# A two-layer decoder trunk in fp32 from split operands: six orders changed, and the first up-projection step's weights made ready early

## The reference, cut to what matters

```
for l in range(2):                                   # x: 1024 prompt rows and 8 x 8 sample rows, D = 1024
    h = x @ w_in[l]                                  # 1792 columns: z_u, z_v, q, k, v
    A = gelu(z_u) * (W_spatial . LN(gelu(z_v)) + b)  # gMLP in chunks of 128 positions
    B = sliding-window attention(rotary(q), rotary(k), v, sinks)   # samples against a cache of 128
    x = LN(alpha * x + concat(A, B) @ w_out[l])
    up = x @ w_up[l]                                 # 2 x 2816 columns, then causal conv of width 3
    x = LN(alpha * x + (gelu(conv(g)) * conv(u)) @ w_down[l])
```

## Time and profile before

| | us |
|---|---|
| median of 3 runs | 2398.47 (2396.57 to 2401.55) |
| the profiled execution | 2398.07 |
| its span in the trace | 2396.3 |
| PE busy | 2244.6 (94%) |
| DVE busy | 1655.8 (69%) |
| ACT busy | 980.8 (41%) |
| POOL busy | 782.8 (33%) |

### The profile page before, as it was taken

How to read it: one execution, slowest core, us unless ns; L and a number is a source line. 1 busy time by engine, 2 the same in 40 slices (tenths; PEclk the granted TensorE clock), 3 DMA queues, 4 the chain that set the end, 5 groups by cost and what they waited for, 6 DMA issues and landing times.

```text
span 2396.3 us, 35859 instructions
## 1 busy us (share of the span) xinstructions
PE 2244.6 (94%) x14276; PEld 2025.5 (85%) x14276; DVE 1655.8 (69%) x2014; ACT 980.8 (41%) x1773; POOL 782.8 (33%) x444
## 2 busy tenths in 40 slices
PE   7999899799999999999999998987999999999996
PEld 7997677699999998887799876767999999987875
DVE  1558747777777776777636586486777777767777
ACT  2227634543443444333412375454344344443332
POOL 1115234434434440220311342344443444402202
PEclk9999989899999999999999999998999999999999
DMA  5412145122222224755551213541222222255762
GB/s 149 99 29 64 57 152 164 45 83 66 73 83 71 68 83 151 276 201 183 188 132 45 56 38 102 144 152 45 65 74 83 69 70 83 83 222 197 249 213 95
DMA packets 207974, 269.50 MB, mean 112 GB/s; under 512 B 31952, under 2 KB 166584, under 8 KB 207736
## 3 DMA queue, kind: packets, MB, share of 16 engines
q1 hardware_dynamic: 207808, 267.21, 36.5%
HBM read 217.39 MB, written 46.13 MB: 110 GB/s over the span
## 4 chain that ended last, share of the span: by engine, by line
PE 56%; DVE 20%; ACT 7%; issue 5%; DMA 4%; POOL 4%; SPq 2%; DVEq 0%; ACTq 0%; POOLq 0%
PE ps L2056 23%; PE ps L1770 13%; PE ps L1735 9%; PE ps L1995 3%; DMA wblk<-in_w_up 3%; DVE rl L1424 2%; POOL bl L733 2%; SPq L528 2%; DVE bnst L1252 1%; DMA wrow<-in_w_down 1%; POOL wblk L741 1%; PE ps L1795 1%; ACT bh L938 1%; PE ps L1874 1%; DVE bl L1356 1%
## 5 line engine op out<-in xcount | busy, mean ns | idle before, releaser
L2056 PE MATMUL ps<-bt,bh 128*128 128x272 f32 x3520 | 598.2, 292 | 29.9 <-issue 19.7
L2056 PEld LDWEIGHTS ps<-bt,bh 128*128 128x128 f32 x3520 | 503.5, 191 | 37.3 <-issue 25.9
L938 ACT ACTIVATE bh<-wblk 128x512 fp32r<-128x512 f32 x308 | 183.6, 624 | 542.8 <-POOL wblk L745 237.5
L2056 PE MATMUL ps<-bt,bl 128*128 128x272 f32 x1760 | 367.3, 290 | 0.0
L1356 DVE TENSOR_TENSOR bl<-wblk,bh 128x512 fp32r<-128x512 f32 x210 | 165.2, 803 | 182.2 <-ACT bh L938 182.2
L2056 PEld LDWEIGHTS ps<-bt,bl 128*128 128x128 f32 x1760 | 278.7, 191 | 0.0
L733 POOL TENSOR_TENSOR bl<-wblk,bh 128x512 fp32r<-128x512 f32 x98 | 163.3, 1669 | 310.8 <-ACT bh L938 310.8
L1770 PE MATMUL ps<-rh,ah 128*128 128x512 f32 x792 | 246.3, 392 | 14.7 <-DVE rzd L1238 6.5
L2056 PE MATMUL ps<-ba,bh 128*128 128x272 f32 x1408 | 238.4, 292 | 9.0 <-POOL bl L733 4.1
L1770 PE MATMUL ps<-rl,ah 128*128 128x512 f32 x792 | 244.1, 389 | 0.0
L1424 DVE TENSOR_TENSOR rl<-wrow,rh 128x1024 fp32r<-128x1024 f32 x132 | 191.6, 1452 | 51.0 <-ACT rh L994 51.0
(11 more groups left out here) (223 smaller groups left out, 4081.4 us busy)
## 6 DMA issues: line engine op xcount, KB each, us to landing
wrow<-in_w_down SPq DMA_DIRECT2D x132, 512.0 KB, 4.7
wblk<-in_w_up SPq DMA_DIRECT2D x88, 512.0 KB, 5.2
a_scr<-hg SPq DMA_DIRECT2D x44, 552.0 KB, 3.4
araw<-a_scr SPq DMA_DIRECT2D x88, 192.0 KB, 4.5
wrow<-in_w_out SPq DMA_DIRECT2D x48, 256.0 KB, 5.5
wrow<-in_w_out SPq DMA_DIRECT2D x24, 512.0 KB, 4.0
wraw<-in_w_in SPq DMA_DIRECT2D x10, 1024.0 KB, 6.0
z_scr<-rzc SPq DMA_DIRECT2D x16, 512.0 KB, 3.7
```

What stands on the lines that cost most here:

```text
L938: act.activation(bh[b][:], block_of(f, b), ACT.Copy).then_inc(S["u_hi"], 1)
L2056: e = nc.tensor.matmul(out[:, n, :], lhs, rhs[:, HW_ // 2 * n:HW_ // 2 * n + HW_ // 2], start=(k == 0 and m == 0), stop=(k == HK - 1 and m ...
```

## The change

Seven things are edited. They change no arithmetic.

1. Samples: the second transposes, the keys and the scores come one block later on PE, the transposes of the probabilities and the values after the first and the second tile of the tail of group 0; ACT's exponentials move from kk = 5 to kk = 6.
2. Norm turns: PE's `turn_z` in groups 1 and 2 comes after kk = 1, 3, 5 instead of 0, 2, 4, and what ACT does with it also one kk later. The product nmr is written as a tensor_scalar.
3. The operands of group 2 on DVE: the next tile's `turned` stands ahead of a tile's `operand_lo`.
4. Keys: the three operations of `keys` stand at gMLP blocks 4, 5 and 6, not all at 5.
5. gMLP: PE does chunk (3, 2) and chunk (4, 0) ahead of block 0's transposes, so each block has the two chunks that follow; the last has one.
6. Residuals: in the down-projection the join of a group's third tile stands ahead of `act_lo` and `down_lo`.
7. Step 0's weights: SP loads them at c = 21 of the output projection into a part of `btf` that tiles 6 and 7 use later. ACT copies B_11 and B_12 at kk = 4 and 5 of group 2; POOL subtracts them after row blocks 20 and 21 and makes two of the four sums after block 22, ahead of block 23. DVE's sums for tiles 6 and 7 wait until those weights are used.

```diff
@@ -369,7 +369,23 @@
+            if f == 0 and b in (B_11, B_12, B_22):
+                return quarter(which, k0)
             return wblk[s0 + which][:, k0:k0 + HK, :]
+
+        def quarter(which, k0):
+
+            return btf[:, 32 - 8 * which + k0:36 - 8 * which + k0, first_cols(NB - 1)]
+
+        def split_of(f, b):
+
+            if f:
+                return bh[b], bl[b]
+            if b < B_S2:
+                r, cols = 32 - 8 * b, first_cols(NB - 2)
+                return bt[:, r:r + HK, cols], bt[:, r + HK:r + 8, cols]
+            i = {B_S2: 0, B_S1: 1, B_S3: 2, B_22: 3, B_S4: 6}[b]
+            return bh[i], bl[i]
...
                 if f == 0:
-                    sp.wait_ge(S["w_lo"], l * WIO + INT + OUTU - 2)
+                    sp.wait_ge(S["c_done"], l * NTOK + 6)
...
-                        elif c < OUTU + 2:
-                            up_cols(l, c - OUTU)
+                        elif c == OUTU:
+                            up_cols(l, 1)
+                        if c == OUTU - 3:
+                            up_cols(l, 0)
...
+            def sum_first(l, b):
...
+                if b == B_S1:
+                    pool.wait_ge(S["wu_landed0"], 32 * (l * (FT // 2) + 1))
+                    pool.tensor_tensor(s1, a21, a22, ALU.add).then_inc(S["u_sum"], 1)
+                elif b == B_S2:
+                    pool.wait_ge(S["u_sum"], n + 1)
+                    pool.tensor_tensor(s2, s1, a11, ALU.subtract).then_inc(S["u_sum"], 1)
...
@@ -788,15 +825,16 @@
                 for c in range(1, OUTU):
                     lo_out(l, c)
-                lo_up(l, 0, B_11)
-                lo_up(l, 0, B_12)
-                for b in (B_S1, B_S2, B_S4):
-                    sum_up(l, 0, b)
-                for b in (B_S2, B_S1, B_22):
+
+                    if OUTU - 4 <= c < OUTU - 2:
+                        lo_up(l, 0, (B_11, B_12)[c - OUTU + 4])
+                    elif c == OUTU - 2:
+                        sum_first(l, B_S1)
+                        sum_first(l, B_S2)
+                sum_first(l, B_S4)
+                sum_first(l, B_S3)
+                for b in SPLIT[2:]:
                     lo_up(l, 0, b)
-                sum_up(l, 0, B_S3)
-                lo_up(l, 0, B_S3)
-                lo_up(l, 0, B_S4)
...
@@ -1106,7 +1147,7 @@
-                            elif kk == 5:
+                            elif kk == 6:
                                 act.wait_ge(S["s_dve"], l * 18 + 13)
@@ -1119,22 +1160,25 @@
                                 normal(l, t1)
-                                turned(l, t0)
                             elif kk == 2:
                                 deviation(l, 0, t2)
                                 normal(l, t2)
+                                turned(l, t0)
+                            elif kk == 3:
                                 operands_hi(l, t0)
-                            elif kk == 3:
+                            elif kk == 4:
                                 turned(l, t1)
-                            elif kk == 4:
+                            elif kk == 5:
                                 operands_hi(l, t1)
-                            elif kk == 5:
+                            elif kk == 6:
                                 turned(l, t2)
-                            elif kk == 6:
+                            elif kk == 7:
                                 operands_hi(l, t2)
                         c = KD * g + kk
                         if c + 2 < OUTU:
                             hi_out(l, c + 2)
+                        if g == 2 and kk in (4, 5):
+                            block_hi(l, 0, (B_11, B_12)[kk - 4])
@@ -1142,19 +1186,19 @@
                 deviation(l, 0, t0)
-                block_hi(l, 0, B_11)
                 normal(l, t0)
-                block_hi(l, 0, B_12)
                 deviation(l, 0, t1)
                 normal(l, t1)
+                block_hi(l, 0, B_S2)
                 deviation(l, 0, t2)
                 normal(l, t2)
+                block_hi(l, 0, B_S1)
                 turned(l, t0)
                 operand_hi(l, t0, 0)
-                block_hi(l, 0, B_S2)
+                block_hi(l, 0, B_22)
                 turned(l, t1)
                 operand_hi(l, t1, 0)
-                block_hi(l, 0, B_S1)
+                block_hi(l, 0, B_S3)
...
@@ -1264,8 +1306,7 @@
-                    dve.scalar_tensor_tensor(out=nmr[0:q, i, :], in0=mv[0:q, i, 0:1], scalar=-1.0, in1=rst[0:q, i, :],
-                                             op0=ALU.mult, op1=ALU.mult).then_inc(S["ln_nm"], 1)
+                    dve.tensor_scalar(nmr[0:q, i, :], mv[0:q, i, 0:1], rst[0:q, i, :], -1.0, ALU.mult, ALU.mult).then_inc(S["ln_nm"], 1)
...
@@ -1302,6 +1343,12 @@
+                    if t == NB - 2:
+
+                        dve.wait_ge(S["u_p"], 7 * l * FT + B_12 + 1)
+                    elif t == NB - 1:
+                        dve.wait_ge(S["u_lop"], lo_n(l, 0, B_22))
+                        dve.wait_ge(S["u_sum"], 4 * l * FT + 4)
...
-                    if b == 5:
-                        keys()
+                    if 4 <= b < 7:
+                        keys(b - 4)
...
@@ -1650,8 +1698,19 @@
-                    for t in C3[g]:
-                        operands(l, t)
+                    if g < 2:
+                        for t in C3[g]:
+                            operands(l, t)
+
+                turned(l, t0)
+                operand_sums(l, t0)
+                for t, following in ((t0, t1), (t1, t2)):
+                    turned(l, following)
+                    dve.wait_ge(S["t_sum"], ts_n(l, t, 2))
+                    operand_lo(l, t, 0)
+                    operand_sums(l, following)
+                dve.wait_ge(S["t_sum"], ts_n(l, t2, 2))
+                operand_lo(l, t2, 0)
...
@@ -1698,6 +1757,7 @@
                         summed(l, 1, 3 * g + 1)
+                        joined_rz(l, 1, 3 * g + 2)
...
-                        summed(l, 1, 3 * g + 2)
+                        moments(l, 1, 3 * g + 2)
...
@@ -1825,12 +1885,14 @@
-                for c in range(3):
-                    in_chunk(3, c)
+                in_chunk(3, 0)
+                in_chunk(3, 1)
                 pe.wait_ge(S["par_ev"], l + 1)
...
+                in_chunk(3, 2)
+                in_chunk(4, 0)
...
-                    for u in (2 * b, 2 * b + 1):
-                        in_chunk(4 + u // 3, u % 3)
+                    for u in (2 * b + 1, 2 * b + 2):
+                        if u < 2 * (NB + 1):
+                            in_chunk(4 + u // 3, u % 3)
...
-                samp = {0: samp_turn, 1: samp_turn2, 2: samp_keys, 3: samp_scores, 5: samp_turned}
+                samp = {0: samp_turn, 2: samp_turn2, 3: samp_keys, 4: samp_scores}
...
-                        elif kk in (0, 2, 4):
+                        elif kk in (1, 3, 5):
                             turn_z(l, C3[g - 1][kk // 2])
...
-                        if g == 0 and i == 0:
-                            samp_values()
+                        if g == 0 and i < 2:
+                            (samp_turned, samp_values)[i]()
```

57 lines of the change are left out of this document (34 added, 23 removed).

## The result

The changed kernel takes 2415.82 us (median of 9 runs, 2407.84 to 2420.25) against 2398.47 of the kernel before in 9 runs beside it: a ratio of 1.0065 (95% interval 1.0055 to 1.0075), or 15.6 us more; the two medians lie 17.4 us apart. That is above the forecast's range of 2382 to 2412. Its profiled execution has a span of 2418.5 us.

What follows compares the result with a forecast made beforehand. PE, 94% busy, bounds the kernel, with idle time in few stretches where the last engine counts, DVE in one. Two layers of +3.0 us, residuals -6.4 and gMLP with keys 0 sum to -0.4: 2398 us, range 2382 to 2412.

Steps and rivals of the forecast that it cites:

- the samples' -5.0: Second transposes of the samples: covered wait and won clock, less a later wait for the probabilities, give -5.0 us a layer.
- the -3.0 between the join of tile 5 and S2: Step 0: nmr clear of POOL's sums -2.0 us, two DVE waits for ACT filled -1.0, in each layer.
- nmr's form: Product nmr as a tensor_scalar: claimed to be no gain by itself, 0 us.
- the later turns: PE's turns of z one block later: -5.0 us in group 1 and -1.7 in group 2, each layer.
- A: Stretch from the output projection to tile 8's wait for DVE in group 1; forecast -5.0 us a layer.
- B: Stretch from tile 8's wait for DVE in group 1 to group 2's third tile; forecast +3.2 us a layer.
- C: Stretch from group 2's third tile to the start of product S2; forecast +5.8 us a layer.
- stall at the start of group 2: Late operand copy on ACT delays DVE's joins and group 2's third tile: +8.2 us, +1.9 of slow clock, each layer.
- rival (3): POOL's queue between row blocks 20 and 23, by turns with DVE: +8 us a layer, 2408 us; chance 0.20.
- Rival (2): Third tile's operand copy does not hold up group 2: 10.1 us less a layer, 2377 us; chance 0.12.
- rival (4): Samples' second transposes still wait 6 us for block 2's POOL subtraction: +10 us, about 2408; chance 0.06.
- rival (1): POOL and DVE avoid each other, tile 5's join moves by +2.3 us alone: total -9.8, 2388 us; chance 0.26.

Runs made afterwards that it cites:

- b4: b1 with the samples' edit taken back: 2383.6 us, ratio 0.9928.
- b1: Kernel before with edits to samples, norm turns, nmr, group 2's operands and residuals, ACT's third-tile operand copy ahead of row block 16's: 2375.5 us, ratio 0.9905.
- f2: Kernel before with only residuals, keys and nmr as a tensor_scalar: 2369.3 us, ratio 0.9883.
- c4: b1 with the product nmr as a scalar_tensor_tensor again: 2381.7 us, ratio 0.9922.
- e2: Changed kernel with ACT's operand copy of the third tile moved ahead of the copy of row block 16: 2395.0 us, ratio 0.9990.
- d4: c1 with the later turns in group 1 only, group 2's turns where they were before: 2367.6 us, ratio 0.9879.
- c1: b1 with the keys' three operations at gMLP blocks 4, 5 and 6 added: 2371.5 us, ratio 0.9891.
- e1: Changed kernel with the edit to step 0's weights undone: 2401.9 us, ratio 1.0017.
- f1: d4 with the edit to group 2's operand order on DVE taken back: 2367.0 us, ratio 0.9869.
- c2: b1 with the gMLP chunk order edit added, keys as before: 2384.9 us, ratio 0.9940.
- d2: c1 with POOL's rotation of q's third block waiting until DVE has normalised the scores of attention's first block: 2372.8 us, ratio 0.9909.
- d1: b2 with POOL's rotation of q's third block waiting until DVE has normalised the scores of attention's first block: 2381.0 us, ratio 0.9935.
- d3: c1 with group 2's operands on DVE in the order of the kernel before: 2373.8 us, ratio 0.9908.
- b2: b1 with the edits to gMLP and keys added: 2384.6 us, ratio 0.9940.
- e4: Changed kernel with POOL's first two sums behind row block 23 instead of ahead of it: 2413.2 us, ratio 1.0070.
- b3: b1 with step 0's weights loaded and copied early, but POOL's subtractions and sums behind the last row block: 2383.3 us, ratio 0.9943.

## Why the prediction was wrong

The number was missed at three places, in each layer: the samples' -5.0, of which 1.6 came; the -3.0 between the join of tile 5 and S2, of which 0.6 came; and gMLP with attention behind it, put at 0, where the changed kernel has +3.7. The first two are gains counted in full that the next waits took back, the third is a cost that no term has. Two larger errors all but cancel, and that is luck: nmr's form, put at 0, gave 9.1 us, and the later turns, put at -6.7, cost 2.5. Each is taken up below.

**The sum, term by term**, per layer:

| term | forecast | measured | by |
|---|---|---|---|
| samples | -5.0 | -1.6 (-4.0 by the medians) | A, b4 to b1 |
| nmr's form | 0 | -9.1 alone, -1.5 to -3 behind later turns | B and C, before to f2; c4 to b1 |
| later turns, group 1 | -5.0 | -0.8 on top of nmr's form | B, f2 to b1 |
| stall at the start of group 2 | +8.2, +1.9 of slow clock | +7.3 to 8.8, +2.3 to 2.6 | B and C, changed to e2 |
| later turns, group 2 | -1.7 | +3.3 | C, d4 to c1 |
| weights, to S2 | a part of +5.6 | +8.1 to 8.9 | C, e1 to changed |
| weights, behind S2 | -1.0 | -2.0 to -2.8 | e1 to changed |
| group 2's operands | -1.0 | -0.5 in C, 0 on the median | f1 to d4 |
| gMLP | 0 | +4.1 to +4.7 | medians, b1 to c2, d2 to d1 |
| keys | 0 | -2, not seen in the trace | medians, b1 to c1 |
| residuals | -3.2 | -3.2 and -3.4 | down-projection, before to changed; never undone alone |

Added up, the measured column is about +7 us a layer, for 7.8 to 8.7 measured in all.

**Right** were the stall at the start of group 2 (a first wait of 4.98 us for "about 5", and the third tile at 11.5 us behind the group's end for 11.6; the two waits between are 0.56 and 1.83 for 2 and 3, because PE took 4.1 us at a granted clock of 0.50 for the eight matmuls there, 2.1 before), its slow clock, PE's wait for block 21, the turns that DVE and POOL take on tile 8's sums, and the residuals. The join of tile 5 came 25.3 us after the start of kk=4, forecast 23.8 with 26.8 as the bound. So rival (3) was the nearer one: it named the place, and gave 8 us a layer without the residuals, where 14 to 15 came; of the 11 to 12 us a layer above the forecast's +3.0, 3.6 are in C, its place, the rest where it names nothing. Rival (2), no stall, falls with the stall itself, rival (4), no gain at the second transposes, with their wait of 2.6 us for 6.3, and rival (1), POOL and DVE out of each other's way, with the 1.1 to 2.4 us that six of tile 8's eight sums of 0.3 us took. Two readings were off without moving the total much. POOL's times, added up again, give block 23 at 19.5 us after the start of kk=4 and not 20.1; it ended at 19.4, and PE waited less than forecast because it came 3.2 us late itself. And the row block of 5.55 us did not run at half clock: the granted clock of its stretch is 0.74. Timelines of DVE and POOL in the changed kernel:

```profile
421.75 1.32 DVE L1359 TENSOR_TENSOR btf<-hT,btf 128x128 f32<-128x128 f32 x1
422.99 2.42 DVE L1361 TENSOR_TENSOR btf<-hT 128x128 f32<-128x128 f32 x1
...
431.15 1.21 DVE L1280 SCALAR_TENSOR_TENSOR rzc<-rzc,ps 128x1024 f32<-128x1024 f32 x1
...
422.88 2.38 POOL L730 TENSOR_TENSOR rl<-wrow,rh 128x1024 fp32r<-128x1024 f32 x1
```

The rule of the Trainium skill that the prediction draws on, "SBUF — State Buffer", "Who interferes with whom", holds in these rows and in those of nmr: by turns throughout the join was to come at 26.8 us behind the start of kk=4, without them at 19.1, and it came at 25.3.

**The step that turned the diagnosis round** is the sentence that nmr's other form "is no gain by itself". It was drawn from one row of another instruction, a TENSOR_SCALAR of 128x8; the operation itself had 18 instances in the trace with a mean of 1271 ns, and it was not looked at. The rule that I had weighed for tile 8 names its case: two SBUF inputs. It hardly moved the total, as the changed kernel has the form too and its gain was booked under the turns, but the waits for the turned copy in groups 1 and 2 were put down to the place of the turns, and the later turns were credited with 6.7 us a layer. Those waits were nmr's. With them gone, the later turns give 0.8 us in group 1, and in group 2 they take 3.3, since tile 8's operands come later and the join of tile 5 with them: a cost that the prediction put at nothing.

**The step that failed for samples** is "one block later 4.2 us of that are covered". They were (6.3 to 2.6), but the values moved by a tile as well, and what is late next, the row operand of tile 8 in group 1, was not worked out. It took back 1.5 of it, and the two waits before the probabilities 1.1, as forecast. Of the 1.8 us of clock counted as won the 1.4 of the block behind the wait never came, since it ran at low clock as before (4.54 us for twelve matmuls, 4.52 before); the transposes ahead of it did take 0.7 us less. In the changed kernel, where that row operand is waited for 2.79 and 3.1 us, A as a whole is 0.5 and 0.1 us shorter in place of 5.0.

**The weights** cost more on the way to S2. The term -3.0 from the join to S2 was too good: it is 27.6 us where it was 28.2, or -0.6. The three products nmr came 1.4 us sooner for the 2.0 forecast. The turned copies took their place in the order, but the first two of the three subtractions of 1.23 us then took 2.19 beside POOL, as in d3's comparison, and ACT's turned copy came later, behind its copies of weight blocks: PE waits 3.15 and 2.59 us for ACT there, where before it waited 1.38 for ACT and 4.21 for DVE, and DVE waits 1.94 for it where it waited 1.42.

**gMLP** was given -3.6 to +1.2. The wait at the last block was priced well (3.37 for 3), but what is behind it was not: low clock on the next product (a granted clock of 0.50 from 168 to 172 us in the changed kernel, 1.00 there before). Runs show +8 to +9 us in two layers. The traces account for some 3 us in the input projection (167.4 and 161.4 with the edit, mean of b2 and d1, against 166.2 and 159.9, mean of c1, d2, d3, d4, f1 and f2) and for up to 4.6 a layer in attention where DVE and POOL meet; with POOL kept away 8.2 us remain on the median. The 3 us are weak, since the input projection of layer 0 is 163.6 us in b1 and 168.4 in b4, by the same code. The runs' mean granted clock points the same way for the whole: 0.973 to 0.974 in b2, c2 and d1, 0.977 to 0.979 in c1 and d2. Between d1 and d2 that is some 17 us more of an execution at the lower of the two levels, which at half speed is about 8 us of PE's work (an estimate from the two means), the size of the loss. Where in the kernel that time lies, and so how the loss splits, is **not settled**: one trace per kernel is too few for a loss that differs between executions.

Taken together, the forecast was too low by 3.6 us a layer at C, 4.7 at A, 3.7 at gMLP and attention and 1.0 at B, and too high by 1.5 behind S2: 11.5 a layer. Twice that, less 0.3 us ahead of the first chunk, is the 22.6 us by which the profiled execution misses it. That execution is the slowest of the changed kernel's nine, with the collision in both layers; on the median the miss is 18 us.

## What to carry to other kernels

Before an order is changed to get round a wait, look at what the releasing engine was doing in front of the release, and sort its instructions by mean duration against their size: here one small product with two SBUF inputs, blocked by GpSimd, made four of the six waits, and its other form gave 18 us in the two stretches where it acts, while the later turns cost 7 in group 2 and gave at most 2 in group 1. Of a step that is moved to cover a wait, follow its own consumer as well: the samples and the later turns in group 2 each covered their wait and were late at the next place. And when several edits are at hand, run the smallest ones first: two of these seven and half of a third, in a few lines, gave 27.7 of the 30 us that the best kernel has.

## What the hardware showed that was not expected

- A scalar_tensor_tensor of 128x1 from two SBUF inputs takes 0.16 us when POOL rests and 2.05 to 2.09 in the eight instances that start 0.3 us after its subtraction of 128x1024 (two of them 64x1); the same product as a tensor_scalar takes 0.21 us in all of 18 instances, POOL or not. A TENSOR_SCALAR of 128x8 did take 1.81 us there, so it isn't the instruction's name alone that decides. What tells the two apart was not tried.
- DVE's sums of 0.3 us beside a busy POOL take 1.1 to 2.4 us each, and neither place that was tried is free of it: with two of POOL's sums behind the last row block (e4) C is within 0.5 us of what it was, and with all of POOL's added work there (b3) it is 5.3 to 6.7 us longer than without.
- The same code gives attention in 98.4 or in 102.7 us, by a difference of 1.1 us in when it starts against POOL's queue. It was seen in 3 layers of the traces of two kernels, never in a kernel without gMLP's edit. In layer 1 of c2 one product takes 2.17 us and attention 99.3. The 100.0 us in layer 1 of b2 are another thing: no such product is long there, but the granted clock of the first 30 us is 0.94.
